# RWKV entry on one core: sums of squares added on VectorE and taken per token, shift rows of the adaptive norm computed with the weights as the moving operand on column tiles

## The reference, cut to what matters

```python
for i in range(DEPTH):                                  # layer 0 is the RWKV layer
    mod = c_act @ ada_w[i] + ada_b[i]                   # c_act = silu(c), one row of 1024
    sh1, sc1, g1, sh2, sc2, g2 = jnp.split(mod, 6, -1)  # six rows of 1024
    h = _rms(x) * (1.0 + sc1) + sh1                     # _rms: x * rsqrt(mean(x*x, -1) + 1e-6)
    y = _rwkv7_mix(h, ...)
...
def _rwkv7_mix(x, mix, w_in, ...):
    xx = _token_shift(x) - x
    xs = x[None] + xx[None] * mix[:, None, None, :]     # six mixtures, for r, w, k, v, a, g
    r = xs[0] @ w_in[:, 0:1024]                         # and five more projections
```

## Time and profile before

| | us |
|---|---|
| median of three runs | 2761.56 (2761.39 to 2763.52) |
| profiled execution, its own time | 2767.65 |
| span of the profiled execution | 2765.8 |
| PE busy in the span | 2558.3 (92%) |
| DVE / ACT / POOL busy | 1193.5 / 979.5 / 977.2 |
| granted clock over the span | 0.962 |

### The profile page before, as it was taken

The page is one execution under the profiler, slowest core; times in us unless marked ns, Lnnn a source line. Parts: engine busy times, 40 slices in busy tenths (PEclk is TensorE's granted clock), DMA queues, the critical chain, the costliest instruction groups (busy, mean ns, idle before and its releaser), DMA issues.

```text
span 2765.8 us, 33536 instructions
## 1 busy us (share of the span) xinstructions
PE 2558.3 (92%) x13896; PEld 1964.2 (71%) x13896; DVE 1193.5 (43%) x1813; ACT 979.5 (35%) x1441; POOL 977.2 (35%) x338
## 2 busy tenths in 40 slices
PE   7996667889999989998999999989899999999899
PEld 5745565368887867876887778869586777666586
DVE  5565884664444262342112443434306424344604
ACT  4652443422322233533332233212324334433523
POOL 2312230634444433443444434413433333222232
PEclk8997897899999998999999999999999999999999
DMA  6121343225554321122224342202122222111121
GB/s 261 62 75 44 90 89 118 77 71 195 190 189 191 137 86 67 47 76 76 95 102 154 135 141 92 92 31 92 44 101 77 95 77 106 61 46 61 39 92 61
DMA packets 92100, 272.09 MB, mean 98 GB/s; under 512 B 54720, under 2 KB 54848, under 8 KB 64320
## 3 DMA queue, kind: packets, MB, share of 16 engines
q1 hardware_dynamic: 89232, 255.03, 26.2%
q10 hardware_dynamic: 2736, 15.21, 1.4%
HBM read 264.44 MB, written 5.78 MB: 98 GB/s over the span
## 4 chain that ended last, share of the span: by engine, by line
PE 79%; DVE 10%; ACT 4%; DMA 2%; issue 2%; POOL 2%; SPq 0%; ACTq 0%; POOLq 0%; DVEq 0%
PE bank L343 20%; PE bank L345 19%; PE bank L344 19%; PE bank L279 2%; PE bank L278 2%; PE bank L277 2%; PE bank L2721 1%; PE bank L3255 1%; POOL ring_low L374 1%; PE bank L3233 1%; DVE conv_out L2447 1%; PE bank L2967 1%; ACT w_high L364 1%; DVE probs L3445 1%; PE bank L790 1%
## 5 line engine op out<-in xcount | busy, mean ns | idle before, releaser
L374 POOL TENSOR_TENSOR ring_low<-ring,w_high 128x2048 fp32r<-128x2048 f32 (+2 forms) x184 | 802.6, 4364 | 1341.8 <-ACT w_high L364 1341.8
L343 PE MATMUL bank<-h_high,w_high 128*128 128x512 f32 (+1 forms) x1304 | 523.3, 401 | 28.2 <-DVE h_low L454 19.9
L345 PE MATMUL bank<-h_high,ring_low 128*128 128x512 f32 (+1 forms) x1304 | 520.1, 399 | 0.0
L344 PE MATMUL bank<-h_low,w_high 128*128 128x512 f32 (+1 forms) x1304 | 517.4, 397 | 0.0
L364 ACT ACTIVATE w_high<-ring 128x2048 fp32r<-128x2048 f32 (+2 forms) x184 | 331.0, 1801 | 357.4 <-PE bank L345 339.9
L343 PEld LDWEIGHTS bank<-h_high,w_high 128*128 128x128 f32 (+1 forms) x1304 | 246.8, 189 | 94.2 <-issue 27.4
L344 PEld LDWEIGHTS bank<-h_low,w_high 128*128 128x128 f32 (+1 forms) x1304 | 246.9, 189 | 60.7 <-issue 0.7
L345 PEld LDWEIGHTS bank<-h_high,ring_low 128*128 128x128 f32 (+1 forms) x1304 | 246.9, 189 | 60.2
L343 PE MATMUL bank<-z_high,w_high 128*128 128x512 f32 x384 | 154.1, 401 | 6.1 <-DVE z_low L3452 2.7
L345 PE MATMUL bank<-z_high,ring_low 128*128 128x512 f32 x384 | 153.5, 400 | 0.0
L344 PE MATMUL bank<-z_low,w_high 128*128 128x512 f32 x384 | 152.6, 398 | 0.0
(11 more groups left out here) (447 smaller groups left out, 4402.0 us busy)
## 6 DMA issues: line engine op xcount, KB each, us to landing
ring<-in_stream SPq DMA_DIRECT2D x194, 1024.0 KB, 4.8
ada_slot<-in_ada_next SPq DMA_DIRECT2D x40, 512.0 KB, 3.2
ada_slot<-in_first SPq DMA_DIRECT2D x8, 1024.0 KB, 5.5
gain_weights<-in_gains ACTq DMA_DIRECT2D x4, 2048.0 KB, 12.0
scale_weights<-in_first SPq DMA_DIRECT2D x4, 1024.0 KB, 19.2
inverse<-scratch_inverse SPq DMA_DIRECT2D x16, 256.0 KB, 4.1
w_first<-in_first SPq DMA_DIRECT2D x2, 1024.0 KB, 7.6
x_res<-in_x SPq DMA_DIRECT2D x2, 1024.0 KB, 11.9
```

The source lines that it names most:

```text
L343: pe.matmul(out, w_high[:, k, cols], x_high, start=start, stop=False)
L344: pe.matmul(out, w_high[:, k, cols], x_low, start=False, stop=False)
L345: return pe.matmul(out, w_low[:, k, cols], x_high, start=False, stop=stop)
L374: pool.tensor_tensor(self.c.ring_low[:, b % SLOTS, 0:cols], self.c.ring[:, b % SLOTS, 0:cols], self.high_buf[:, b % 2, 0:cols].bitcast(F32 ...
```

## The change

**Sums of squares.** ACT squares as before. DVE adds tiles 1 to 6 onto tile 0 in place (six additions, each waiting for the last by a semaphore). PE then multiplies the sum and tile 7, as stationary 128x128 pieces (4 pieces of 128 tokens each), with one column of ones: eight matmuls with one moving column, giving the sum of squares token-major in a 128x4 corner of a bank. ACT's root and DVE's reciprocal act on 128x4. PE spreads the result back to 128 rows by 512 tokens with four matmuls (the column, broadcast, stationary; the identity moving) into bank 5, and `unit_tile` reads it there. `keep_warm` puts eight 128x128 matmuls ahead of it all and two behind the sums.

**Shift rows.** A block's eight matmuls now have a column of silu(c), broadcast to 32 columns, as stationary operand and the 128x256 weights as moving one; tile k goes to the column group k % 4, so four partial rows land on four groups of 32 partitions. ACT copies the 128x256 result to SBUF (`copy_shift`), and two matmuls with one moving column `pick` (ones at partitions 0, 32, 64, 96, made by a reduction of the identity) add the four partials and turn the row into two columns. DVE adds the bias as before.

```diff
+    rstd, tok = chip.bank[5][:, :], lambda j: slice(j * P, (j + 1) * P)
...
+        def shift_rows_of(i):
             chip.wait_block(pe, b_sh + i)
-            pe.wait_ge(silu.sem, silu.of(1))
-            if i == 3:
-                pe.wait_ge(shift.sem, shift.of(0))
+            if i == 0:
+                pe.wait_ge(silu.sem, silu.of(1))
+            if i >= 2:
+                pe.wait_ge(shift_copy.sem, shift_copy.of(i - 2))
...
+            for k in range(KD):
+                mm = pe.matmul(chip.bank[6 - 2 * (i % 2)][head_group(k), 0:2 * P],
+                               c_col[:, k:k + 1].to_broadcast([P, 32]), w[:, k, :], start=(k < 4), stop=(k >= 4))
+            mm.then_inc(shift_rows.sem, 1)
+            pe.wait_ge(shift_rows.sem, shift_rows.of(i))
+            pe.sem_inc(chip.gemm_done, 2)
+
+        def shift_columns(i):
+            pe.wait_ge(shift_copy.sem, shift_copy.of(i))
+            if i:
+                pe.wait_ge(shift.sem, shift.of(i - 1))
             for j in range(2):
...
+                mm = pe.matmul(chip.bank[7][:, j:j + 1], shift_row(i)[:, tok(j)], pick, start=True, stop=True)
...
+        chip.keep_warm(pe, 8, 3)
+        pe.wait_ge(added.sem, added.of(KD - 3))
+        for j in range(ST):
+            pe.matmul(chip.bank[4][:, j:j + 1], v_mix[:, 0, tok(j)], chip.ones[:, 0:1], start=(j == 0), stop=False)
+        pe.wait_ge(squared.sem, squared.of(KD - 1))
...
+        chip.keep_warm(pe, 2, 3)
+        pe.wait_ge(inverse.sem, inverse.of(0))
+        for j in range(ST):
+            mm = pe.matmul(chip.bank[5][:, tok(j)], rstd_cols[:, j:j + 1].to_broadcast([P, P]), chip.ident[:, :],
+                           start=True, stop=True)
+        mm.then_inc(spread_rstd.sem, 1)
+        pe.wait_ge(picked.sem, picked.of(0))
+        shift_rows_of(0)
+        shift_rows_of(1)
+        shift_columns(0)
+        shift_columns(1)
...
+            if k == 1:
+                shift_rows_of(2)
+                shift_columns(2)
             if k == 2:
-                shift_block(3)
+                shift_rows_of(3)
+                shift_columns(3)
...
+        copy_shift(0)
+        copy_shift(1)
         for k in range(2):
             norm(k)
         for k in range(2):
             mix("r", k)
         for k in range(KD):
             round_mix("r", k)
+            if k == 1 or k == 2:
+                copy_shift(k + 1)
             if k + 2 < KD:
                 norm(k + 2)
                 mix("r", k + 2)
...
+        for k in range(1, KD - 1):
+            dve.wait_ge(squared.sem, squared.of(k))
+            if k > 1:
+                dve.wait_ge(added.sem, added.of(k - 2))
+            dve.tensor_tensor(v_mix[:, 0, :], v_mix[:, 0, :], v_mix[:, k, :], ALU.add).then_inc(added.sem, 1)
+        dve.wait_ge(root.sem, root.of(0))
+        dve.reciprocal(rstd_cols, rstd_cols).then_inc(inverse.sem, 1)
+        dve.wait_ge(spread_rstd.sem, spread_rstd.of(0))
+        unit_tile(0)
         dve.wait_ge(silu.sem, silu.of(0))
         scale_pair(0)
-        dve.wait_ge(root.sem, root.of(0))
-        dve.reciprocal(rstd, rstd).then_inc(inverse.sem, 1)
-        dve.wait_ge(inverse.sem, inverse.of(0))
-        unit_tile(0)
         shift_pair(0)
```

More of the change, by code:

```diff
@@ L196, in take_groups, with keep_warm @@
         return u
+    def keep_warm(self, pe, n, bank=7):
+        for _ in range(n):
+            pe.matmul(self.bank[bank][:, 0:P], self.ident[:, :], self.ones[:, :], start=True, stop=True)
     def slot(self, b, kt):
@@ L713, in rwkv_project @@
     chip.limit = SBUF
+    ST = T // P
     f = chip.rwkv = Rwkv(chip)
@@ L723, in rwkv_project @@
     h, shifted = lambda k: hz[:, k, 1:T + 1], lambda k: hz[:, k, 0:T]
-    rstd, rn, sigma = tmp[:, 0, :], tmp[:, 0, :], lambda n: tmp[:, n % 2, :]
+    rn, sigma = tmp[:, 0, :], lambda n: tmp[:, n % 2, :]
+    shift_row, rstd_cols, pick = lambda i: tmp[:, 0, i % 2 * 2 * P:(i % 2 + 1) * 2 * P], tmp[:, 1, 0:ST], tmp[:, 1, 8:9]
+    rstd, tok = chip.bank[5][:, :], lambda j: slice(j * P, (j + 1) * P)
     squares = lambda n: tmp[:, n % 6, :]
@@ L751, in rwkv_project @@
     first_rounded, first_rest = Step(chip, "rw_first_rounded", 2), Step(chip, "rw_first_rest", 2)
-    squared, mean, root, inverse = (Step(chip, "rw_norm", n) for n in (KD, 1, 1, 1))
-    unit, shift_mm, shift = Step(chip, "rw_unit", KD), Step(chip, "rw_shift_mm", 4), Step(chip, "rw_shift", 4)
+    squared, added, mean, root, inverse, spread_rstd = (Step(chip, "rw_norm", n) for n in (KD, KD - 2, 1, 1, 1, 1))
+    picked, unit = Step(chip, "rw_picked", 1), Step(chip, "rw_unit", KD)
+    shift_rows, shift_copy = Step(chip, "rw_shift_rows", 4), Step(chip, "rw_shift_copy", 4)
+    shift_mm, shift = Step(chip, "rw_shift_mm", 4), Step(chip, "rw_shift", 4)
     summed, scale, normed = Step(chip, "rw_summed", 8), Step(chip, "rw_scale", 4), Step(chip, "rw_normed", KD)
@@ L798, in tensor @@
-        for k in range(KD):
-            pe.wait_ge(squared.sem, squared.of(k))
-            mm = pe.matmul(chip.bank[4][:, :], chip.ones[:, :], v_mix[:, k, :], start=(k == 0), stop=(k == KD - 1))
-        mm.then_inc(mean.sem, 1)
-        for i in range(3):
-            shift_block(i)
+            for k in range(KD):
+                mm = pe.matmul(chip.bank[6 - 2 * (i % 2)][head_group(k), 0:2 * P],
+                               c_col[:, k:k + 1].to_broadcast([P, 32]), w[:, k, :], start=(k < 4), stop=(k >= 4))
@@ new lines, in tensor @@
+        pe.wait_ge(added.sem, added.of(KD - 3))
[3 more added lines that the diff above has]
+        for j in range(ST):
+            mm = pe.matmul(chip.bank[4][:, j:j + 1], v_mix[:, KD - 1, tok(j)], chip.ones[:, 0:1],
+                           start=False, stop=(j == ST - 1))
+        mm.then_inc(mean.sem, 1)
+        chip.keep_warm(pe, 2, 3)
@@ L905, in scalar, with copy_shift @@
         act.wait_ge(mean.sem, mean.of(0))
-        act.activation(rstd, chip.bank[4][:, :], ACT.Sqrt, bias=chip.eps[:, :], scale=1.0 / D).then_inc(root.sem, 1)
+        act.activation(rstd_cols, chip.bank[4][:, 0:ST], ACT.Sqrt, bias=chip.eps[:, :], scale=1.0 / D)\
+           .then_inc(root.sem, 1)
         act.wait_ge(one_less.sem, one_less.of(1))
+        def copy_shift(i):
+            act.wait_ge(shift_rows.sem, shift_rows.of(i))
+            act.activation(shift_row(i), chip.bank[6 - 2 * (i % 2)][:, 0:2 * P], ACT.Copy)\
+               .then_inc(shift_copy.sem, 1)
         def norm(k):
@@ L1049, in rest @@
                .then_inc(x_rest.sem, 1)
+        dve.tensor_reduce(pick, chip.ident[:, 0:P:32], AX_X, ALU.add).then_inc(picked.sem, 1)
+        for k in range(1, KD - 1):
[7 more added lines that the diff above has]
+        unit_tile(0)
         dve.wait_ge(silu.sem, silu.of(0))
         scale_pair(0)
[L1053 to L1056 removed]
         shift_pair(0)
```

10 lines of the change are left out of this document (1 added, 9 removed).

## The result

The changed kernel takes 2776.41 us (median of 5 runs, 2772.15 to 2779.27); five runs of the kernel before on the same chip gave 2762.7 (2761.39 to 2763.59). The ratio is 1.0043, 95% interval 1.003 to 1.0055. On a second chip, 11 runs beside 34 of before gave 1.0026 (1.0017 to 1.0034). Both intervals lie above 1, so it is slower, by 7 to 12 us. The profiled execution took 2772.15 with a span of 2770.4 at a clock of 0.963: 4.5 us more than the one of before.

What follows compares the result with a forecast made beforehand. It took the first phase's entry as the bound, through the time of tile 6's norm and PE's clock at 69.46; 5.3 + 5.3 + 3.3 - 4.2 - 1.6 = +8.1 on 2761.56 gave 2769.7 us, range 2764 to 2777.

Steps and rivals of the forecast that it cites:

- Term 1: Entry, new sums through shift rows: the first norm starts at 33.75 instead of 28.45 us, +5.3.
- Term 2: ACT's copy of shift row 2 ahead of tile 3's norm: norm at 48.5 instead of 37.89, +5.3 more.
- Term 3: ACT's copy of shift row 3 ahead of tile 4's norm: norm at 57.4 instead of 43.50, +3.3 more.
- Term 4: DVE's old wait for shift block 3 ahead of tile 6's norm goes away, -4.2 us.
- Term 5: PE's restart at tiles 6 and 7: tile 5's matmuls already bring the clock up, -1.6 us.
- The sum: All five terms of the first phase together, +8.1 us, giving 2769.7 us.
- DVE keeps its turn: Rival: POOL gets in only after six short additions; first norm near 29.3, sum +3.7, 2765.3 us; chance 0.2.
- The entry is really shorter: Rival: early shift rows, ACT never stands at copies; first norm 25.7, sum -8.5, 2753 us; chance 0.06.
- The clock stays low: Rival: entry matmuls don't lift PE's clock; first norm +6.8, sum +15.1, 2776.7 us; chance 0.18.

Runs made afterwards that it cites:

- e8: The changed kernel again, unedited, on the chip of the other runs; ratio 1.0026 to the kernel before.
- e1: The changed kernel, with POOL's second subtraction of the first weights waiting for the last of DVE's six additions; ratio 1.0019 to the kernel before.
- e12: e7 with only ACT's copy of shift row 3 moved behind the norm and part of tile 2, PE's order unchanged; ratio 0.9973 to the kernel before.
- e7: e3 with ten warming matmuls in place of eight, waiting for the second square so they run just ahead of the sums; ratio 0.9977 to the kernel before.
- e6: Sums, root and reciprocal of the kernel before, with the new shift rows, rows 2 and 3 and copies early; ratio 0.9971 to the kernel before.
- e2: The changed kernel with shift rows 2 and 3 ahead of the r matmuls, their copies beside tile 0's rounding; ratio 1.0004 to the kernel before.
- e3: The changed kernel with the edits of both e1 and e2; ratio 0.9995 to the kernel before.

## Why the prediction was right, step by step

- **Term 1** (+5.3): +4.7. The first addition ended at 15.31 and the second took 4.82, the sixth ended at 23.41 (23.4 foretold); the sums were there at 27.06 (27.0), `unit_tile` began at 29.83 (29.7). The missing 0.6 us is in the shift rows, which were done before DVE's scale pair (33.0, as foretold) and so no longer set the first norm. PE in the changed kernel, then in `e8`:

```profile
29.72 1.08 PE L800 MATMUL bank<-ring,c_col 128*32 128x256 f32 x16
30.99 1.07 PE L800 MATMUL bank<-ring,c_col 128*32 128x256 f32 x16 [0.19 <-PE bank L800]
```

```profile
29.76 1.94 PE L800 MATMUL bank<-ring,c_col 128*32 128x256 f32 x16
31.88 1.63 PE L800 MATMUL bank<-ring,c_col 128*32 128x256 f32 x16 [0.18 <-PE bank L800]
```

  In the first, row 0 already ran at full clock; in the second, the same program, it ran at half, and the first norm came at 34.57, near the 35.2 given for a clock that stays low. So the clock's price was sized rightly, and whether it is paid differs between executions. Two readings behind this term need a word. The profile gives a granted clock of 1.00 for the first 25 us of the kernel before, while the weight loads of L800 took 0.34 us up to 17.80 and 0.19 behind it; the prediction went by the durations, and the changed kernel's sums at 0.50 bear it out. And the 0.43 us for a plain fp32 instruction of 512 columns is a row of another kind in the earlier trace rows; the loads of L800 from 18.54 on, one every 0.43 us, give the same number at full clock, so the sum stands.
- **Term 2** (+5.3): 48.05 - 37.89 = 10.2, less term 1's 4.7, is +5.4.
- **Term 3** (+3.3): +4.5. I took most of tile 2's twelve matmuls at half clock, 4.4 us in all; all of them were, 5.4 us, and row 3 took 1.36 instead of 1.1. The windows of PE (PE, PEld, DVE, ACT, POOL busy, clock, DMA share, GB/s):

```profile
44.00:50.00 6.00, 4.30 (x32) 2.80 (x30) 0.55 (x2) 2.20 (x4) 0.00 (x0) 1.00 0.15 34
50.00:52.00 2.00, 0.96 (x2) 0.83 (x3) 2.00 (x3) 0.12 (x1) 0.00 (x0) 0.57 1.00 422
52.00:56.00 4.00, 4.00 (x11) 2.98 (x9) 2.10 (x7) 0.00 (x0) 0.00 (x0) 0.50 0.01 2
```

- **Term 4** (-4.2): from tile 4 to tile 6 the gap to before went from 14.7 to 10.5, -4.1.
- **Term 5** (-1.6): PE restarted 10.5 late, at full clock, and its first matmul on the next block of r, at 76.70 before, came at 85.96, 9.3 late: -1.2.
- **The sum** (+8.1): +9.3 at that point and +7.5 at the phase's end. The last step, -1.8, I had not foreseen. 1.6 of it lie at one place: PE waits 2.61 us for a POOL subtraction in both kernels, and of these two only in the kernel before did the clock fall at it. The kernel before, then after:

```profile
124.06 0.67 PE L343 MATMUL bank<-mix_high,w_high 128*128 128x512 f32 x1 [2.61 <-POOL ring_low L374]
```

```profile
133.40 0.50 PE L348 MATMUL bank<-mix_high,w_high 128*128 128x512 f32 x1 [2.61 <-POOL ring_low L379]
```

So the forecast for the phase was 0.6 us off, and that is luck in part: term 3 was 1.2 too small, term 1 0.6 too large, and the clock at the late stall, which no term had, took 1.6 off. At the stall itself the gap was 9.3 us against the 8.1.

The rivals. "DVE keeps its turn" put the first norm at 29.3 and the sum at +3.7; `e1` made it true and gave 29.69 and +4.4, so it was priced well and did not happen. "The entry is really shorter" needs copies that never wait: it failed on the order of the lists, as the prediction said, and `e12` with another order comes near it: -7.4, 1.6 of it the clock at the late stall, against -8.5, with a first norm at 27.88 and not 25.7. "The clock stays low" was wrong as a whole, since the clock was full by tile 1's matmuls (44 to 50 us above); its number, 2776.7, is nearer to the measured 2776.41 than mine, but not for its reason: the phase grew by 7.5, not 15.1. That the measured time lies inside the range at all is owed to this rival, which set the upper end 0.6 us above it: between the medians on one chip the change cost 13.7 us where I forecast 8.1. The rest of the 13.7 us is no part of the entry that these runs show, and its cause stays open; the second chip's ratio, 1.0026 or 7.2 us, agrees with the entry's 7.5 to 7.9.

By the Trainium skill ("SBUF — State Buffer", on the two sides) a VectorE instruction with two SBUF inputs and a GpSimd instruction that reads SBUF exclude each other for a whole instruction; `e1` agrees, 4.69 us for the six additions against 8.80. The Trainium skill ("TensorE: Matmul & The Clock Gate", the table of why this matters) also wants no idle gaps between bursts of matmuls, by which the early warm-up is spent. This case agrees: the first eight one-column instructions took 1.86 us in the changed kernel, 17.84 us behind its warm-up, and 1.05 in `e7`.

## What to carry to other kernels

An instruction on a strictly ordered engine that waits for a late result costs all that stands behind it: before adding one, compare the time at which its input is ready with the time at which its successor could start, and move the one instruction rather than the whole group (norm of tile 6 at 50.82 with only the copy moved, at 53.80 with the row as well). Work that leaves TensorE for VectorE costs more than its own time where it ends the stream that kept TensorE's clock up (shift block 0: 6.83 us against 3.63), and more again where GpSimd can take a turn between the new instructions (4.7 us). Try each half of a two-part change alone: here the half that saves TensorE time (the wide rows) is worth 0.3% in the right place, and the other half costs time as it stands and, repaired, gives nothing that these runs can tell from zero (`e12` against `e6`).

## What the runs showed of the hardware

Whether the clock falls at a short stall is not a matter of its length alone. The four microseconds from the end of the same stall of 2.61 us, in the windows of the kernel before and of the changed one:

```profile
124.00:128.00 4.00, 3.94 (x10) 3.12 (x11) 2.71 (x1) 3.10 (x5) 3.29 (x2) 0.57 0.33 137
```

```profile
133.30:137.30 4.00, 3.90 (x17) 3.20 (x18) 2.67 (x1) 3.14 (x5) 3.29 (x2) 1.00 0.40 168
```

PE is busy for 3.94 and 3.90 us, and before and after it the same instructions stand, but the clock is 0.57 in one and 1.00 in the other. The stall stands in all fourteen profiles, 2.60 to 2.65 us long: the four microseconds behind it have a clock of 1.00 in five (the changed kernel, `e8`, `e2`, `e3`, `e12`) and of 0.50 to 0.66 in the other nine. Nine matmuls took 3.75 us in the kernel before and 2.19 in the changed one, which is the 1.6 us above. What decides it is not shown. The clock also differs later, where the program is the same: two executions of the changed kernel, 7.5 and 7.9 us behind at the phase's end, ended with spans of 2770.4 and 2780.4. One of the stretches between, of the first profile and of the second:

```profile
450.00:500.00 50.00, 40.64 (x578) 27.40 (x574) 20.26 (x38) 19.04 (x41) 5.83 (x9) 0.80 0.23 86
```

```profile
450.00:500.00 50.00, 40.64 (x513) 27.39 (x512) 17.81 (x32) 17.67 (x38) 4.27 (x7) 0.70 0.23 86
```

PE is busy for 40.64 us in both, at a mean clock of 0.80 and 0.70. So a difference of spans of single executions says nothing here below some 10 us. The phase's own end agreed to 0.4 us in these two, and can hold the 1.6 us of the stall.

Sixteen column-tiled instructions of 256 columns took 1.07 us at full clock and 1.94 at half, as estimated from the 512-column row; the 32 one-column ones that they replace took 3.63 and 6.96. And GpSimd got its turn after a single VectorE addition here: the first ran 0.71 us, the second was held 4.82. Each addition waits for the last by a semaphore; whether that gap is what lets GpSimd in is argued and not shown.
